# Low-rank input products in sequence, the variance's root as a step of its own, and the last product by tokens

## The reference

```
a = rms_norm(h, g_mix);  p = a @ w_in
# RWKV branch: q = p * sb[0] + token_shift(p) * sb[1], split into r, k, v, xw, xa, xg
w  = -softplus(-(w0 + tanh(xw) @ w_lora_w)) - 0.5
aa = sigmoid(a0 + xa @ a_lora_w);  g = sigmoid(xg) @ g_lora_w      # xw, xa, xg: 64 + 64 + 160 columns of p
o  = scan(r, exp(-exp(w)), k, v, kk, aa)                           # 16 heads of 64
var = mean(square(o - mu));  o = (o - mu) * rsqrt(var + 64e-5)     # per head and token
...
h = h + mixed @ w_out
f = rms_norm(h, g_ffn)
h = h + square(relu(f @ w_ffn1)) @ w_ffn2                          # 1024 -> 4096 -> 1024
return rms_norm(h, g_final)
```

## Time and profile before

| what | value |
|---|---|
| median of 3 runs | 3664.14 us (3653.7 to 3667.68) |
| the profiled execution | 3669.2 us, of which the span from first to last instruction is 3667.4 us |
| PE busy | 3607.2 us (98%), 22028 matmuls |
| DVE, ACT, POOL busy | 1794.8 us (49%), 1314.8 us (36%), 331.5 us (9%) |
| mean granted TensorE clock | 0.987 of full speed |

### The profile page before, as it was taken

The page is one execution under the profiler, slowest core; times in us unless marked ns, Lnnn a source line. Parts: engine busy times, 40 slices in busy tenths (PEclk is TensorE's granted clock), DMA queues, the critical chain, the costliest instruction groups (busy, mean ns, idle before and its releaser), DMA issues.

```text
span 3667.4 us, 51198 instructions
## 1 busy us (share of the span) xinstructions
PE 3607.2 (98%) x22028; PEld 2956.3 (81%) x22028; DVE 1794.8 (49%) x2465; ACT 1314.8 (36%) x2009; POOL 331.5 (9%) x328
## 2 busy tenths in 40 slices
PE   9999999999999999999999999999999999899998
PEld 8888888877788887888888888887877777688887
DVE  5435434455543455443444354345657767655444
ACT  5545222344432232332235453224332333443222
POOL 2011101100110111110010111012000000000001
PEclk9999999999999999999999999999999999899999
DMA  7213232321333332332332123333312222532322
GB/s 228 75 55 92 95 98 92 98 70 55 95 95 97 95 99 87 101 98 92 101 95 70 55 87 100 98 92 90 110 51 73 77 57 71 179 109 89 103 91 74
DMA packets 334229, 338.08 MB, mean 92 GB/s; under 512 B 12097, under 2 KB 324019, under 8 KB 333747
## 3 DMA queue, kind: packets, MB, share of 16 engines
q1 hardware_dynamic: 333714, 334.72, 29.8%
q10 hardware_dynamic: 288, 0.09, 0.0%
HBM read 320.07 MB, written 14.68 MB: 91 GB/s over the span
## 4 chain that ended last, share of the span: by engine, by line
PE 94%; DVE 4%; ACT 2%; issue 1%; ACTq 0%; POOLq 0%; POOL 0%; DVEq 0%
PE P L99 92%; PE P L102 2%; ACT sA L114 1%; DVE lo L117 0%; DVE rw_S L117 0%; DVE ds L125 0%; DVE vg L125 0%; ACT rw_k L114 0%; ACTq L160 0%; ACT hi L113 0%; DVE x L117 0%; DVE sA L125 0%; DVE rw_k L125 0%; DVE rw_S L125 0%; DVE rw_kk L117 0%
## 5 line engine op out<-in xcount | busy, mean ns | idle before, releaser
L99 PE MATMUL P<-aH,lo 128*128 128x512 f32 x2840 | 1134.2, 399 | 9.9 <-DVE rw_S L117 5.0
L99 PE MATMUL P<-aH,hi 128*128 128x512 f32 x2840 | 1109.9, 391 | 0.0
L99 PE MATMUL P<-aL,hi 128*128 128x512 f32 x2840 | 1109.7, 391 | 0.0
L113 ACT ACTIVATE hi<-raw 128x1024 fp32r<-128x1024 f32 (+2 forms) x617 | 611.4, 992 | 1037.3 <-PE P L99 1032.7
L117 DVE TENSOR_TENSOR lo<-raw,hi 128x1024 fp32r<-128x1024 f32 (+2 forms) x617 | 748.7, 1230 | 232.6 <-ACT hi L113 232.5
L99 PEld LDWEIGHTS P<-aH,lo 128*128 128x128 f32 x2840 | 535.6, 189 | 139.8 <-issue 17.8
L99 PEld LDWEIGHTS P<-aH,hi 128*128 128x128 f32 x2840 | 535.2, 188 | 113.5
L99 PEld LDWEIGHTS P<-aL,hi 128*128 128x128 f32 x2840 | 535.4, 189 | 112.4 <-issue 5.3
L99 PE MATMUL P<-bH,lo 128*128 128x512 f32 x1088 | 423.5, 389 | 1.6 <-DVE hold L117 1.6
L99 PE MATMUL P<-bL,hi 128*128 128x512 f32 x1088 | 423.3, 389 | 0.0
L99 PE MATMUL P<-bH,hi 128*128 128x512 f32 x1088 | 423.3, 389 | 0.0
(11 more groups left out here) (303 smaller groups left out, 3852.2 us busy)
## 6 DMA issues: line engine op xcount, KB each, us to landing
raw<-in_w_ffn_in_dram SPq DMA_DIRECT2D x176, 512.0 KB, 3.6
raw<-in_w_in_dram SPq DMA_DIRECT2D x163, 512.0 KB, 3.9
raw<-in_w_ffn_out_dram SPq DMA_DIRECT2D x96, 384.0 KB, 3.1
raw<-in_w_ffn_dram SPq DMA_DIRECT2D x36, 512.0 KB, 3.8
raw<-in_w_o_dram SPq DMA_DIRECT2D x26, 512.0 KB, 3.4
raw<-in_w_ffn_dram SPq DMA_DIRECT2D x32, 384.0 KB, 3.4
raw<-in_w_mem_kv_dram SPq DMA_DIRECT2D x16, 512.0 KB, 6.4
raw<-in_w_ffn_out_dram SPq DMA_DIRECT2D x16, 512.0 KB, 3.5
```

The lines of the kernel that those rows point to most:

```text
L99: return self.e.matmul(out, l, r, start=start, stop=stop, skip_group_check=skip) if self.e else Nothing()
L113: return self.e.activation(out, in_, func, scale=scale)
```

## The change

Three places are changed.

1. The low-rank jobs: `abreast` (unit 0 of `lora`, `lora2`, unit 1 of `lora`) becomes `jobs_steps` (`lora`, then `lora2`), with banks 0, 3 and 2 instead of 0, 1 and 2. `norm` and `first_mean` come after six `mm` steps (36 matmuls) instead of eight (48), and `first_mean` no longer pulls an eviction ahead of itself.
2. `rw_var` keeps the PE part; Ln and Exp on ACT become `rw_root`, a step of its own, with planned latencies 0.7 and 1.5 instead of 1.6.
3. The last down-products get form "W": activations stationary, 512 weight columns moving, output 128 tokens x 512 features in a bank, four tiles (all four banks of the ring) for each half of the features, units of at most two 128-row blocks. They are added to `m["xt"][q]`, x by tokens, which the new step `turn_x` makes: 4 transposes on PE and 4 copies of 128 columns on ACT for each of 8 tiles, one step in every eight `mm` steps from the tenth on. The last norm is by tokens: ACT squares with a sum along the row, Ln and Exp on one column, and DVE scales by root and gain; the gain is fetched once, to all partitions. `norm(11)` and `finish`'s transposes and copies go; the stores are eight, of 128 tokens x 512 features.

In the diff the branch `post == "last"` is ACT's `evict`, and the branch `post in ("tokens", "last")` is DVE's.

```diff
-        jobs.append(Job(("down", l, f0), W2, l, 0, D, parts, last if done else "add", norm=after))
+        if last == "last":
+            jobs.append(Job(("down", l, f0), W2, l, 0, D, parts, last if done else "tokens", width=512, form="W", arg=f0))
+        else:
+            jobs.append(Job(("down", l, f0), W2, l, 0, D, parts, last if done else "add", norm=after))
...
-    out += [vec("rw_out", dve=0.7, gap=0.5, hold=True), Step("rw_var", p, u, pe=0.9, lat=1.6),
+    out += [vec("rw_out", dve=0.7, gap=0.5, hold=True), Step("rw_var", p, u, pe=0.9, lat=0.7), Step("rw_root", p, u, lat=1.5),
...
-    lora = abreast([Job("lora", ("w_in_2", 0), "r", C_LORA, 256, a, "lora", norm=9, arg=0),
-                       Job("lora2", ("w_in_2", 0), "r", C_LORA + 256, 128, a, "lora", width=128, norm=9, arg=2)])
-    stage([0, 1, 2, 3], lora[:8] + [Step("norm", 9), Step("first_mean")] + lora[8:])
+    lora = jobs_steps([Job("lora", ("w_in_2", 0), "r", C_LORA, 256, a, "lora", norm=9, arg=0, bank=[0, 3]),
+                       Job("lora2", ("w_in_2", 0), "r", C_LORA + 256, 128, a, "lora", width=128, norm=9, arg=2, bank=[2])])
+    stage([0, 1, 2, 3], lora[:6] + [Step("norm", 9), Step("first_mean")] + lora[6:])
...
+    for k in range(KT):
+        main.insert(10 + 8 * k, Step("turn_x", k, pe=0.45))
+    stage([0, 1, 2, 3], main[:8] + [Step("norm", 10), Step("last_gain")] + main[8:])
+    stage([0], [Step("finish")])
...
-            if s.name not in ("norm", "mem_norm"):
+            if s.name not in ("norm", "first_mean", "mem_norm"):
                 order += later
...
+            elif job.form == "W":
+                o, ah, al = bank(b), H[:, a0 + k, 128 * mi:128 * mi + 128], L[:, a0 + k, 128 * mi:128 * mi + 128]
+                e.mm(o, al, hi[:, k, :], first, False)
+                e.mm(o, ah, lo[:, k, :], False, False)
+                t = e.mm(o, ah, hi[:, k, :], False, last)
...
+        elif post == "last":
+            j, q, mean, root = cg // 512, tile, st[:, 20 + tile:21 + tile], st[:, 16 + tile:17 + tile]
+            x = m["xt"][q][:, 512 * j:512 * j + 512]
+            e.wait_ge(*S.evict.at(key))
+            if j:
+                e.wait_ge(*S.act_turn.at(("square sum", 0, q)))
+            e.act(m["scr"][:, q, :], x, ACT.Square, accum=st[:, 8 + 4 * j + q:9 + 4 * j + q]).then_inc(*S.act_turn.up(("square sum", j, q)))
+            if j:
+                e.wait_ge(*S.evict.at(("mean of half", q)))
+                e.wait_ge(*S.act_turn.now())
+                e.act(root, st[:, 12 + q:13 + q], ACT.Ln, 1.0 / D, mean).then_inc(*S.act_turn.up())
+                e.wait_ge(*S.act_turn.now())
+                e.act(root, root, ACT.Exp, -0.5).then_inc(*S.act_turn.up(("root", q)))
+                e.wait_ge(*S.act_turn.now())
+                e.wait_ge(*S.evict.at(("scaled", q)))
+                if q == 3:
+                    first = m["xt"][q][:, 0:512]
+                    e.act(first, first, ACT.Copy, root).then_inc(*S.act_turn.up(("y", 0, q)))
...
+        elif post in ("tokens", "last"):
+            j, q = cg // 512, tile
+            x = m["xt"][q][:, 512 * j:512 * j + 512]
+            if job.arg == 0:
+                e.wait_ge(*S.act_evict.at(("x by token", 4 * j + 3)))
+            else:
+                e.wait_ge(*S.evict.at(written["tokens", q, j]))
+            if post == "last" and j and q == 0:
+                scale_half(3)
+            e.tt(x, x, o, ALU.add).then_inc(*S.evict.up(key))
+            written["tokens", q, j] = key
+            if post == "last" and not j and q:
+                scale_half(q - 1)
+            if post == "last" and j:
+                for qq in {2: (0,), 3: (1, 2, 3)}.get(q, ()):
+                    last_half(qq)
...
+    def scale_half(q):
+        x = m["xt"][q][:, 0:512]
+        e.wait_ge(*S.last_in.at(0))
+        e.wait_ge(*S.act_turn.at(("square sum", 0, q)))
+        e.ts(st[:, 20 + q:21 + q], st[:, 8 + q:9 + q], 1.0 / D, 1e-6, ALU.mult, ALU.add).then_inc(*S.evict.up(("mean of half", q)))
+        e.tt(x, x, m["gain_by_token"][:, 0:512], ALU.mult).then_inc(*S.evict.up(("scaled", q)))
+
+    def last_half(q):
+        x, root = m["xt"][q], st[:, 16 + q:17 + q]
+        e.wait_ge(*S.act_turn.at(("root", q)))
+        e.stt(x[:, 512:1024], x[:, 512:1024], root, m["gain_by_token"][:, 512:1024], ALU.mult, ALU.mult).then_inc(*S.evict.up(("y", 1, q)))
+        if q < 3:
+            e.ts(x[:, 0:512], x[:, 0:512], root, None, ALU.mult).then_inc(*S.evict.up(("y", 0, q)))
```

More of the change, by code:

```diff
@@ L199, in job_steps @@
         tiles = job.width // 128 if job.form == "T" else job.ntok
-        cols = 0.227 * 3 if job.form == "T" else 0.120 * 3
+        cols = 0.120 * 3 if job.form == "N" else 0.227 * 3
         if job.form == "T" and job.norm == "mem":
@@ L527, in the_order @@
                 order += [("split_high", unit[key] + AHEAD), ("split_low", unit[key] + AHEAD - 1)]
-            tile = (job.name, cg, mi if job.form == "T" else mi // 2)
+            tile = (job.name, cg, mi // 2 if job.form == "N" else mi)
             if tile not in bank:
@@ L691, in mm @@
         last_part = pi == len(job.parts) - 1
-        if pi == 0 and ka == 0 and (job.form == "T" or mi % 2 == 0):
+        if pi == 0 and ka == 0 and (job.form != "N" or mi % 2 == 0):
             take(b)
@@ L720, in mm @@
                 t = e.mm(o, ah, hi[:, k, :], False, last, True)
-        if last_part and kb == kc and (job.form == "T" or mi % 2):
-            tile = mi if job.form == "T" else mi // 2
+        if last_part and kb == kc and (job.form != "N" or mi % 2):
+            tile = mi // 2 if job.form == "N" else mi
             signals.append((job.name, cg, tile))
@@ L1130, in sgu_mix, with turn_x @@
         freed[b] = (S.evict, ("sgu_biased", g))
[L1132 to L1140, removed]
+    def turn_x(k):
+        b = 4 + k % 2
+        e.wait_ge(*S.evict.at(("x", 10, k)))
+        take(b)
+        for q in range(4):
+            t = e.tp(P[:, b, 128 * q:128 * q + 128], m["x"][:, k, 128 * q:128 * q + 128], ident)
+        t.then_inc(*S.turned.up(("x by token", k)))
+        freed[b] = (S.act_evict, ("x by token", k))
     todo = dict(load_mem=load_mem, turn_rows=turn_rows, load_x=load_x, norm=norm, first_mean=first_mean, mem_norm=mem_norm,
@@ L1547, in sgu_inverse, with turn_x @@
         e.act(a[:, :, 2], a[:, :, 2], ACT.Exp, -0.5).then_inc(*S.act_turn.up("ln"))
[L1549 to L1553, removed]
+    def turn_x(k):
+        e.wait_ge(*S.turned.at(("x by token", k)))
+        for q in range(4):
+            t = e.act(m["xt"][q][:, 128 * k:128 * k + 128], P[:, 4 + k % 2, 128 * q:128 * q + 128], ACT.Copy)
+        t.then_inc(*S.act_evict.up(("x by token", k)))
     todo = dict(load_mem=load_mem, load_x=load_x, norm=norm, mem_norm=mem_norm, mem_lambda=mem_lambda, mem_scores=mem_scores, mem_turn=mem_turn,
@@ L2268, in load_x_back, with last_gain @@
         e.dma(m["x"][:, :, :], d["spill"].rearrange("p (k n) -> p k n", n=S_)).then_inc(*S.x_back.up(0, by=16))
+    def last_gain():
+        e.wait_ge(*S.evict.at(("ln", 3, 1)))
+        e.dma(m["gain_by_token"][:, :], d["g_final_2"].rearrange("(a n) -> a n", a=1).to_broadcast([128, D])
+              ).then_inc(*S.last_in.up(0, by=16))
     def finish():
-        o = d["out"][0].rearrange("(t p) d -> p t d", p=128)
-        for k in range(1, KT, 2):
-            e.wait_ge(*S.act_evict.at(("y", k)))
-            e.dma(o[:, :, 128 * k - 128:128 * k + 128], m["y"][:, :, 128 * k - 128:128 * k + 128]).then_inc(*S.out.up(k, by=16))
+        for q in range(4):
+            for j in (1, 0):
+                e.wait_ge(*(S.act_turn if j == 0 and q == 3 else S.evict).at(("y", j, q)))
+                e.dma(d["out"][0, 128 * q:128 * q + 128, 512 * j:512 * j + 512], m["xt"][q][:, 512 * j:512 * j + 512]
+                      ).then_inc(*S.out.up(by=16))
         e.wait_ge(*S.out.now())
@@ L2391, in memory_map @@
     m["hold"] = [m["hold0"][:, :], m["hold1"][:, :]]
-    at("y", [4, D], off=big)
+    for q, off in enumerate((ex, ex + 4096, aH + 16384, aL + 16384)):
+        at(f"xt{q}", [D], off=off)
+    m["xt"] = [m[f"xt{q}"] for q in range(4)]
+    at("gain_by_token", [D], off=kv)
     return m
```

26 lines of the change are left out of this document (9 added, 17 removed).

## The result

The changed kernel takes 3645.2 us (median of 6 executions, 3635.8 to 3648.5) where the kernel before takes 3664.1: a ratio of 0.9945, interval [0.9932, 0.9959], 18.9 us less. The forecast was 3648.0. It was right in time and range; its terms were each a little off, in both directions, and the clock gave something that the sum didn't have.

What follows compares the result with a forecast made beforehand. PE at 98% busy bounds the kernel. Low-rank inputs 6.7, roots 3.9 and last product 5.5 sum to 16.1 us, taking the median from 3664.1 to 3648.0 us; range 3637 to 3659.

Steps and rivals of the forecast that it cites:

- Low-rank inputs, 6.7: First k projection's bank: removing PE's 4.97 us wait and 1.70 of cold products saves 6.7 us; bounds 0 to 6.7.
- The needs worked out beside it: Low-rank inputs: other things PE needs (means, lx, lo, small transfers) would be ready in time, so no wait replaces the old.
- The roots, 3.9: Ends of rounds 1 and 4: both 1.99 us waits for squares go, saving 3.9 us; bounds 0 to 5.5.
- that chain starts from ACT's second Exp, which also comes 2 us earlier, so I count 1.9: Round 4: PE's later 1.57 us wait for a bank would end earlier too, so 1.9 us is gained.
- rival (a): Waits move instead of going, at low-rank inputs or rounds; about half of 10.6 us lost, 3653 us; chance 0.12.
- The last product, 5.5: Down-products by tokens: tail 19.4 to 9.9 us, 9.5 less, minus 4.0 for transposes, gives 5.5 us.
- rival (c): Form W of the last product is slower per matmul or its banks are held; 3671 us at 30 ns; chance 0.05.
- rival (b): Transposes in the last product's stream do not overlap with products, costing 9.6 us instead of 4.0; 3654 us; chance 0.06.
- so DVE sets the pace: New tail: roots 1 to 3 are ready at 2.0, 3.3 and 4.4, so DVE's passes decide, ending at 6.0.
- from 3647.98, when the last product is there: Old tail: counted from 3647.98 to the span's end at 3667.4, 19.4 us.
- rival (d): More comes from the clock: all six waits gone and 2 to 5 us of clock, 3640 us; chance 0.17.
- shorter waits may keep it up: End of round 4: clock granted at 0.54 of 2.4 GHz might stay higher with shorter waits, 2 to 5 us.

Runs made afterwards that it cites:

- lora_banks: Kernel before with its old low-rank order, only the banks changed (0 and 3, then 2); last addition to x to end of round 1 159.5 us, before 168.6.
- root_only: Kernel before with only Ln and Exp of the variance made a step of its own; 3652.8 us, ratio 0.9966.
- before_pad5: Kernel before with five useless copies of the variance's product added ahead of the second stream's sum in round 1; 3658.7 us, ratio 0.9983.
- root_pad2: Kernel before with the root's own step, plus two useless copies of the variance's product in round 1; 3654.6 us, ratio 0.9973.
- tokens_only: Changed kernel with the low-rank and root edits taken back, leaving the last product by tokens; 3660.7 us, ratio 0.9987.
- whole_again: The changed kernel run once more with no edit; 3643.5 us, ratio 0.9937 against the kernel before.
- turn_twice: Changed kernel with every group of the last stage's transposes issued twice, 32 transposes more; 3646.2 us, ratio 0.9952.
- last_two: Changed kernel with the last product's last chunk as one part of ten blocks, so the last unit has two blocks; 3638.5 us, ratio 0.9936.

## Why the prediction was right, and where not

**Low-rank inputs, 6.7: right, slightly more.** 6.9 us in the stretch that the sum was made for (the kernels that keep the wait take 31.0 to 32.5 us there, those without it 24.4), 8.0 by the end of the round. The wait and the slow products behind it both went. The needs worked out beside it had the room that was claimed, and `lora_banks` shows that they had more: with the last `lx` ready 5 us later PE still doesn't wait.

**The roots, 3.9: 2.9 for the waits, and the clock on top.** Round 1 gave 2.0 for the wait itself, and nearly as much again that the sum left out. Behind the wait the kernel before runs cold, as behind the wait for `rw_S` (PE's timeline of before):

```profile
2705.84 0.86 PE L99 MATMUL P<-aH,lo 128*128 128x512 f32 x1
...
2709.89 0.40 PE L99 MATMUL P<-aH,lo 128*128 128x512 f32 x1
```

Nine products take 4.05 us, in after 2.45 (2693.32 to 2695.77). For the low-rank inputs the prediction priced such products (1.70), here it counted only the wait; in `root_only` the stretch is 2.3 us shorter, in after 3.9 (18.2 to 14.3). In round 4 the step that failed is "that chain starts from ACT's second Exp, which also comes 2 us earlier, so I count 1.9". The second Exp does; the chain doesn't start from it. Compare `before_pad5` and `root_pad2`, DVE and ACT behind round 4. In the first:

```profile
3121.45 0.75 DVE L125 SCALAR_TENSOR_TENSOR rw_r<-rw_r,v,rw_k 128x512 f32<-128x512 f32 x1
...
3126.01 4.90 DVE L117 TENSOR_TENSOR bL<-o,bH 128x512 fp32r<-128x512 f32 x8
...
3131.97 1.28 DVE L117 TENSOR_TENSOR hold<-P,R 128x512 f32<-128x512 f32 x2
```

and in the second:

```profile
3113.59 0.75 DVE L125 SCALAR_TENSOR_TENSOR rw_r<-rw_r,v,rw_k 128x512 f32<-128x512 f32 x1 [1.87 <-ACT rw_k L114]
...
3117.95 4.90 DVE L117 TENSOR_TENSOR bL<-o,bH 128x512 fp32r<-128x512 f32 x8
...
3123.90 1.28 DVE L117 TENSOR_TENSOR hold<-P,R 128x512 f32<-128x512 f32 x2
```

The first squares are at 3116.46 and 3109.33. The second stream's root is ready 7.3 us behind them in one and 5.5 in the other, 1.9 earlier as forecast. But DVE is not: it is at the first stream's three passes until 6.4. Before, those were done while PE and ACT were still at the second root, and hid under the wait; now both streams' six passes run one after another, and `bL` starts at 8.6 instead of 9.55, `hold` at 14.6 instead of 15.5. PE gets to that place at 11.9 (15.7 in `before_pad5`, where part of the way went at a lower clock) and waits 3.4 us there. To its restart it is 15.3 us instead of 16.2: 0.9 in place of 1.9. That is rival (a) for half of one term, measured against the shortest of the kernels with the wait; the others of them take 17.2 to 18.3, most of them at a lower clock.

**The last product, 5.5: 5.2, by two errors that nearly cancel.** Form W runs at 389 ns with no wait, so rival (c) falls. The transposes cost 0.47 a group, 3.8 in all (4.0); rival (b), 9.6, falls with the doubled groups. The new tail is 9.0 and not 9.9: the stores took 3.6 us (3630.5 to 3634.1; forecast 3.5), but the last pass ended at 5.4 and not 6.4. The step that failed is "so DVE sets the pace". It added durations, 0.75 + 0.49; on DVE the next pass starts before the last one's end, 0.66 and 0.40 from start to start in the tail (3627.45, 3628.12, 3628.51), 1.06 a tile. ACT was given 1.1 to 1.3 a tile without the accumulator's read of 0.19, and takes 1.32.

The old tail was misread. The prediction's "from 3647.98, when the last product is there" names DVE's addition of the last tile but one; the last matmul and the last addition of the kernel before are these (PE's and DVE's timelines):

```profile
3648.91 0.39 PE L99 MATMUL P<-bH,hi 128*128 128x512 f32 x1
...
3649.34 0.69 DVE L117 TENSOR_TENSOR x<-x,P 128x512 f32<-128x512 f32 x1 [0.67 <-PE P L99]
```

From the product's end, 3649.3, to 3667.4 are 18.1 us and not 19.4. So the tail gave 18.1 - 9.0 = 9.1, less 3.8 for the groups 5.3, and `tokens_only` shows 5.2. The stage is 6.5 shorter in after. That difference goes with the root's step, not with the last product: the last stage takes 477.4 to 478.0 us in the seven kernels with the old last product and the old root, 475.8 and 476.4 in the two with the new root; by tokens it takes 472.8 with the old root and 471.4 to 471.5 with the new one (after, `whole_again`, and `turn_twice` less its 4.0). In its first 36 us the mean clock is 0.67 to 0.72 in the eight kernels with the old root and 0.72 to 0.81 in the six with the new. Why the mixing keeps a higher clock behind the new root isn't shown.

**The sum.** The stretches give 8.0 + 2.9 + 5.2 = 16.1 us. That this is the forecast to the tenth is luck: the terms were off by 1.3 up, 1.0 down and 0.3 down. The time fell by 18.9 and 22.1. The 3 to 6 us beyond are rival (d), the clock, which the sum had at nothing. Behind the removed waits "shorter waits may keep it up" is what the traces have (some 2 us in round 1), and the last stage has 1.3 us more. At the ends of rounds 2 and 4 it is not shown: in the kernel before these steps stand at 1.2 GHz in the profiled execution, in the changed kernel one of them (`whole_again`) or neither (after, `turn_twice`, `last_two`), but adding work by a few us in front of them does that as well as removing waits. What decides between the levels at a given position stays open; the runs show only that work added in front changes how often the low one comes, that the waits need not change for it, and that one program has both (`whole_again` and after).

## What to carry to other kernels

Price a removed wait with the slow products behind it, at the next thing that the engine needs, and follow that need back to the instruction that really starts it: two chains may pass through the instruction that moved, and only one may begin there. When a bank is what is waited for, try giving the bank away before reordering its readers. And where small steps run near the clock's edge, first measure what adding a little useless work does: if that makes the kernel faster, a gain of that size behind an edit may not be the edit's own.

## What the runs showed of the hardware

- 4.4 us of added products made a kernel of 3665.6 us 7 us faster (0.9983 [0.9973, 0.9992]), with the granted clock over the last 18 us of rounds 2 and 4 at 1.00 instead of 0.52 and 0.59 in the profiled executions.
- Behind a wait of 1.99 us nine products of 512 columns took 4.05 us, without the wait 2.45. The whole place took 14.3 to 16.0 us without it and 18.2 to 20.3 with it, in five traces each.
- The same program on the same input had round 2 in 139.4 us at full clock and in 145.3 with its last 18 us at 0.54.
- A square with a sum on ACT has a second instruction behind it, 0.19 us, that reads the accumulator; four of them stand in a row in the tail.
- A transpose of 128x128 that lasts 0.27 us costs 0.11 in a stream of products.
